# Level products of a chunked gated scan: 64 moving columns in place of 128

## What is computed

```python
def _hgrn2_chunk_scan(q, k, v, log_f):
    """S_t = diag(f_t) S_{t-1} + k_t v_t^T ; o_t = S_t^T q_t."""
    ...
        cum = jnp.cumsum(gi, axis=2)
        o_inter = jnp.einsum('bhtk,bhkv->bhtv', qi * jnp.exp(cum), state)
        diff = cum[:, :, :, None, :] - cum[:, :, None, :, :]
        decay = jnp.exp(jnp.where(causal[:, :, None], diff, -jnp.inf))
        scores = jnp.einsum('bhtk,bhtsk,bhsk->bhts', qi, decay, ki)
        o_intra = jnp.einsum('bhts,bhsv->bhtv', scores, vi)
```

## Time and profile before

| | |
|---|---|
| median of three executions | 3034.97 us |
| the profiled execution, its own time | 3036.25 us |
| its span | 3034.3 us |
| TensorE: matmul records (PE), weight-load records (PEld) | 2937.1 us (97%), 2478.7 us (82%) |
| DVE, ACT, POOL busy | 1331.6, 869.1, 221.3 us |
| mean granted TensorE clock | 0.986 of full speed |

### The profile page before, as it was taken

How to read it: one execution, slowest core, us unless ns; L and a number is a source line. 1 busy time by engine, 2 the same in 40 slices (tenths; PEclk the granted TensorE clock), 3 DMA queues, 4 the chain that set the end, 5 groups by cost and what they waited for, 6 DMA issues and landing times.

```text
span 3034.3 us, 36527 instructions
## 1 busy us (share of the span) xinstructions
PE 2937.1 (97%) x15532; PEld 2478.7 (82%) x15532; DVE 1331.6 (44%) x1674; ACT 869.1 (29%) x1275; POOL 221.3 (7%) x168
## 2 busy tenths in 40 slices
PE   7999999989999999997999999999998999999999
PEld 5888989768888888876988978888876888888887
DVE  6343343555445554336421575674245333333332
ACT  4333343432221111235221243343123222211111
POOL 2121111210000000014100000000011000000000
PEclk8999999999999999998999999999999999999999
DMA  3101101213334432121322301002131111111111
GB/s 121 34 29 36 36 29 36 84 35 118 118 118 125 127 124 69 48 64 63 134 63 70 104 21 35 29 21 91 49 97 35 49 49 49 49 49 49 49 49 63
DMA packets 206450, 198.50 MB, mean 65 GB/s; under 512 B 6224, under 2 KB 187856, under 8 KB 206288
## 3 DMA queue, kind: packets, MB, share of 16 engines
q1 hardware_dynamic: 206288, 196.16, 20.7%
HBM read 182.51 MB, written 13.63 MB: 65 GB/s over the span
## 4 chain that ended last, share of the span: by engine, by line
PE 89%; DVE 5%; ACT 3%; issue 1%; POOL 0%; DMA 0%; SPq 0%; ACTq 0%; DVEq 0%; POOLq 0%
PE ps L399 15%; PE ps L402 15%; PE ps L415 14%; PE ps L603 7%; PE ps L594 7%; PE ps L596 7%; PE ps L485 3%; PE ps L440 3%; PE ps L444 3%; PE ps L442 3%; PE ps L762 2%; DVE HT L1392 2%; PE ps L733 1%; PE ps L745 1%; PE ps L765 1%
## 5 line engine op out<-in xcount | busy, mean ns | idle before, releaser
L1374 DVE TENSOR_TENSOR Wlo<-Wraw,Whi 128x1024 fp32r<-128x1024 f32 x220 | 272.3, 1242 | 1083.4 <-ACT Whi L954 1083.4
L954 ACT ACTIVATE Whi<-Wraw 128x1024 fp32r<-128x1024 f32 x232 | 244.1, 1058 | 1451.3 <-PE ps L415 735.4
L399 PE MATMUL ps<-Hh,Whi 128*128 128x512 f32 x1888 | 595.3, 397 | 23.3 <-ACT Hh L983 14.1
L402 PE MATMUL ps<-Hh,Wlo 128*128 128x512 f32 x1888 | 589.6, 394 | 0.0
L415 PE MATMUL ps<-Hl,Whi 128*128 128x512 f32 x1856 | 453.4, 394 | 4.3 <-DVE Hl L1789 4.2
L399 PEld LDWEIGHTS ps<-Hh,Whi 128*128 128x128 f32 x1888 | 354.8, 190 | 107.6 <-ACT Hh L983 15.8
L402 PEld LDWEIGHTS ps<-Hh,Wlo 128*128 128x128 f32 x1888 | 359.7, 191 | 76.1
L415 PEld LDWEIGHTS ps<-Hl,Whi 128*128 128x128 f32 x1856 | 348.9, 189 | 81.3 <-DVE Hl L1789 5.6
L594 PE MATMUL ps<-ah,Whi 128*128 128x512 f32 x1024 | 398.8, 389 | 1.2 <-ACT ah L1124 1.2
L596 PE MATMUL ps<-ah,Wlo 128*128 128x512 f32 x1024 | 398.4, 389 | 0.0
L603 PE MATMUL ps<-al,Whi 128*128 128x512 f32 x1024 | 253.4, 389 | 0.1
(11 more groups left out here) (259 smaller groups left out, 3379.2 us busy)
## 6 DMA issues: line engine op xcount, KB each, us to landing
Wraw<-in_m_w SPq DMA_DIRECT2D x128, 512.0 KB, 3.9
n<-in_w_ada SPq DMA_DIRECT2D x64, 512.0 KB, 3.6
Wraw<-in_w_in SPq DMA_DIRECT2D x56, 512.0 KB, 4.1
R<-in_xT SPq DMA_DIRECT2D x16, 512.0 KB, 5.0
Wraw<-in_w_gate SPq DMA_DIRECT2D x16, 512.0 KB, 4.5
Wraw<-in_w_out SPq DMA_DIRECT2D x8, 512.0 KB, 4.2
xs_scratch<-R SPq DMA_DIRECT2D x8, 512.0 KB, 3.2
Wraw<-in_dft_d SPq DMA_DIRECT2D x8, 512.0 KB, 4.2
```

What stands on the lines that cost most here:

```text
L399: e.matmul(t[:, c], wh[:, k, ms], opd.hi[:, k, c], start=k == 0, stop=False)
L402: e.matmul(t[:, c], wl[:, k, ms], opd.hi[:, k, c], start=False, stop=False)
L954: e.activation(Whi[n % 4][:], Wraw[n % 2][:], ACT.Copy).then_inc(*S("w_hi").tick(n))
L1374: e.tensor_tensor(Wlo[n % 4][:], Wraw[n % 2][:], Whi[n % 4][:].bitcast(F), ALU.subtract).then_inc(*S("w_lo", "v").tick(n))
```

## The change

Levels 1 to 5 and level 6 become one form: for each of the 8 chunks all 128 keys are the stationary operand, and only the 64 queries of the second halves of the blocks, picked by a strided view (`later`), are the moving one. The products fill 512 columns of PSUM in place of 1024. The masked copies of levels 1 to 5 read 256 columns per call in place of 512, with the same columns of the mask, and write to the second halves in `acc`. Level 6 computes 128 keys by 64 queries per chunk in 8 products in place of 16 small ones, and ACT picks its rectangles out of the wider tile. Levels 0 and 7 stay.

```diff
--- before.py
+++ after.py
@@ -199,6 +199,10 @@
         mc = lambda m0, w0=0: (lambda k: mods[:, m0 + k, w0:w0 + 1])
         c3 = lambda t: t[:].rearrange("p (c m) -> p c m", m=128)
 
+        def later(t, m):
+
+            return t.rearrange("p (b two m) -> p b two m", two=2, m=m)[:, :, 1, :]
+
 
         def cols128(w, c0, rows=1024, r0=0):
             return w[r0:r0 + rows, c0:c0 + 128].rearrange("(k p) c -> p k c", p=P)
@@ -480,14 +484,12 @@
                 else:
                     pe.wait_ge(S("q_mul").at((h, lev - 1)), S("q_copy").at((h, lev - 1)))
                     pe.wait_ge(S("k_mul").at((h, lev - 1)), S("k_copy").at((h, lev - 1)))
-                if m < 32:
+                if lev == 0:
                     for c in range(8):
                         i = e.matmul(c3(ps)[:, c, :], K[:, c, :], Q[:, c, :], start=True, stop=True)
-                elif m == 32:
-                    for b0 in (0, 64):
-                        for c in range(8):
-                            i = e.matmul(ps[b0:b0 + 32, 32 * c:32 * c + 32], K[:, c, b0:b0 + 32],
-                                         Q[:, c, b0 + 32:b0 + 64], start=True, stop=True)
+                elif m <= 32:
+                    for c in range(8):
+                        i = e.matmul(ps[:, 64 * c:64 * c + 64], K[:, c, :], later(Q[:, c, :], m), start=True, stop=True)
                 else:
                     for c in range(8):
                         i = e.matmul(ps[0:64, 64 * c:64 * c + 64], K[:, c, 0:64], Q[:, c, 64:128], start=True, stop=True)
@@ -1058,7 +1060,7 @@
                         act.wait_ge(full_at(("level", h, lev)), out_at(("level", h, 5), 1))
                         for p, b0 in enumerate((0, 64)):
                             e.activation(a3_[b0:b0 + 32, :, b0 + 32:b0 + 64],
-                                         ps[b0:b0 + 32, 0:256].rearrange("p (c t) -> p c t", c=8),
+                                         ps[b0:b0 + 32, 0:512].rearrange("p (c t) -> p c t", c=8)[:, :, 32 * p:32 * p + 32],
                                          ACT.Copy).then_inc(*freed(("level", h, lev), p))
                     elif m == 64:
                         act.wait_ge(full_at(("level", h, lev)), out_at(("level", h, 6), 1))
@@ -1487,8 +1489,17 @@
                                 dve.wait_ge(full_at(("tail", h - 1, 2)))
                             else:
                                 dve.wait_ge(S("acc_zero").at(0))
-                            e.copy_predicated(c3(acc)[:, c, :], masks[:, lev, :][:, None, :].broadcast_to([P, 4, P]),
-                                              c3(ps)[:, c, :]).then_inc(*freed(("level", h, lev), p))
+                            if lev:
+                                nb = T // (2 * m)
+                                to = acc[:].rearrange("p (b two m) -> p b two m", two=2, m=m)
+                                to = to[:, nb // 2 * p:nb // 2 * (p + 1), 1, :]
+                                which = later(masks[:, lev, :], m)[:, None, :, :].broadcast_to([P, 4, nb // 8, m])
+                                to = to.rearrange("p (c b) m -> p c b m", c=4)
+                                of = ps[:, 256 * p:256 * p + 256].rearrange("p (c b m) -> p c b m", c=4, m=m)
+                            else:
+                                to, of = c3(acc)[:, c, :], c3(ps)[:, c, :]
+                                which = masks[:, lev, :][:, None, :].broadcast_to([P, 4, P])
+                            e.copy_predicated(to, which, of).then_inc(*freed(("level", h, lev), p))
                 elif kind == "tail" and i == 1:
                     s3, ps = c3(St), c3(tile(("tail", h, 1)))
                     dve.wait_ge(full_at(("tail", h, 1)))
```

## The result

| | before | with the change |
|---|---|---|
| median | 3036.93 us (11 executions, 3034.79 to 3039.63) | 3043.69 us (11 executions, 3041.46 to 3045.78) |
| ratio, with its 95% interval | | 1.0023 (1.0013 to 1.0032) |
| profiled execution, span | 3034.3 us | 3042.8 us |

The change makes the kernel slower, by 6.8 us between the medians, 4 to 10 us by the interval. Against the three executions known ahead of the prediction, the forecast of 3040.2 us stood for +5.2 us. The measured 3043.7 us lies in the stated range of 3027.5 to 3046.7 us, and in the part of it that belongs to the load as the bound (3036.8 to 3046.7).

A forecast was written before the change was run, and what follows sets the result against it. TensorE was taken to bound the kernel, with pairs bound by the 128-column load. Terms 0 + 5.2 + 0 + 0 = +5.2 us on the three executions' median of 3034.97 gave 3040.2 us, range 3027.5 to 3046.7.

The forecast's parts named there:

- What bounds a pair: TensorE's load and matmul pairs: cost is the longer stream, not the sum; a 128-column load takes about 107 ns.
- The slope of the load records: Load records on TensorE grow 113, 138, 192 ns with width, 0.78 to 0.84 ns a column.
- The pairs with 64 stationary columns: Four pairs with 128 moving columns take 0.44 us, 110 ns each, the price of 128 and 128.
- The third row: Behind level 6, the first full-width pair's matmul of 0.39 us ends 0.11 us later, taken as standing for its load.
- Levels 1 to 5 at 0 us: 40 blocks of 16 pairs stay at 111.5 ns a pair with 64 moving columns: 0 us.
- One of the signs: In blocks of levels 1 to 5 after the change, matmul records near 222 ns would show the prediction right.
- Level 6 at +5.2 us: Level 6's wider products add 0.56 us in four heads, 0.75 in heads 1, 3, 5, 0.7 in head 7.
- The estimate of 473 ns: Each of 80 masked copies in levels 1 to 5 falls from 744 ns to this; 22 us less DVE time, hidden.
- The bound of 744 ns: Upper bound for a halved masked copy, if a stepped view costs double per column; the lower was 372.
- The moving columns as the price: Rival: pairs in levels 1 to 5 cost 67 ns, as at level 7; -28.9 us, 3006.1 us; chance 0.11.
- the mixture: Rival: a pair costs something in between, say 95 ns; -7.5 us, 3027.5 us; chance 0.05.
- The clock: Rival: half-streamed blocks lower the granted clock in head 7; +16.5 us on +5.2, 3056.7 us; chance 0.06.

The follow-up runs named there:

- the second execution of the change: Profiled execution from measuring the unaltered changed kernel again beside the kernel before; that run took 3043.62 us beside 3035.88, ratio 1.0026.
- the kernel with one load for two levels: Kernel before, with odd raw queries and level 2's queries moving over one load, level 1 without own products; 3024.50 us beside 3035.11, ratio 0.9962.

## Why the prediction was right

**What bounds a pair.** The step on which all hung, that the load of 128 columns is the longer stream at 107 ns and the moving side is hidden behind it, held. It rested on three rows, and two of them bore it. The slope of the load records held: inside a block a pair takes 112 ns at 64 and at 32 moving columns, and 58 when the load is halved too, which is 0.84 ns for each stationary column, the slope of the records, and 5 ns on top of the 107 and 53 that the slope alone gives. (The prediction's own 67 ns for level 7 is 1.07 us divided by 16, with the ends of the block in it, and would not have lain on its line.) The pairs with 64 stationary columns held too: 109 ns in the scan. The third row, the matmul behind level 6, was misread. Its record of 0.39 us isn't that of a matmul that stands for its load because little streamed ahead of it: behind 128 stationary and 32 moving columns the record is 0.36 us (at 74.01), the same as behind 128 and 128 (at 75.77), and behind 64 stationary and 128 moving ones it is 0.39. It goes with the narrower stationary operand.

The Trainium skill gives, in TensorE: Matmul & The Clock Gate, section LDWEIGHTS (loading the stationary operand), the columns divided by 1.2 ns, 107 for 128 and 53 for 64 columns; the measured pairs take 5 ns more than that at both widths. The formula in its section Back-to-back issue gap counts the moving columns alone, but the section calls it the gap of isolated matmuls and says that in a stream of load and matmul pairs both set the spacing, which the prediction left out. The runs agree with that: with 128 stationary columns the moving ones, from 128 down to 32, don't change the 112 ns.

**Levels 1 to 5 at 0 us.** Right, and as put: a pair stays at 112 ns, and from projection to projection an even head's block takes 2.02 us for 2.03. In an odd head the projections behind a block give back 0.06 for its 0.05. One of the signs was wrong: I looked for matmul records near 222 ns and they are 275, as long as if 128 columns streamed.

**Level 6 at +5.2 us.** Right: 0.55 us in an even head (0.56), 0.70 in an odd one (0.75), and alone it takes as long as the whole change. The scan holds 5.3 us of the median's 6.8, and the interval takes both in. That three runs gave 6.8, 7.7 and 7.0 us and none less than 5.2 has no account in the prediction; it is no part of what was right.

**The sign.** The chances put 0.62 on a change within 0.2% and 0.23 on slower. The measured ratio is just outside 0.2%. The mechanism that I called the likeliest was there, and in the scan nothing beside it; what set slower against the same was 1 us of the sum at a line of 6.1, with a scatter of the clock between executions that is larger. On which side of the line the result fell was luck.

**The masked copies.** The estimate of 473 ns for each was wrong for two levels out of five, and cost nothing, because it is hidden. The timeline of DVE in head 0 (start, us for two copies), levels 0, 1 and 3:

```profile
70.27 1.38 DVE L1502 COPY_PREDICATED acc<-masks,ps 128x512 f32<-128x512 uint8 x2 [7.89 <-PE ps L489]
...
74.88 1.36 DVE L1502 COPY_PREDICATED acc<-masks,ps 128x256 f32<-128x256 uint8 x2 [0.40 <-PE ps L492]
...
84.20 0.77 DVE L1502 COPY_PREDICATED acc<-masks,ps 128x256 f32<-128x256 uint8 x2 [2.79 <-PE ps L492]
```

In levels 3 to 5, which write runs of 4, 8 and 16 elements of `acc`, two copies take 0.77 to 0.79 us, about what was forecast. In levels 1 and 2, with runs of 1 and 2, half the elements take the full time (1.36 and 1.35 us for two). The bound of 744 ns, given for a stepped view at double the price per column, was the value there. The mean record is 577 ns, and 80 x 167 ns are 13 us of records; as busy time the masked copies go from 66.3 us to 51.3, 15 us less and not 22.

DVE as a whole is only 5.5 us less busy (1326.1 for 1331.6), which the prediction didn't see coming. The gate products of q became longer, before (first line) and after:

```profile
L1477 DVE TENSOR_TENSOR q<-q,Tb 128x512 f32<-128x512 f32 x48 | 34.8, 725 | 8.0 <-PE ps L489 8.0
```

```profile
L1479 DVE TENSOR_TENSOR q<-q,Tb 128x512 f32<-128x512 f32 x48 | 45.4, 945 | 11.8 <-PE ps L492 11.8
```

With the shorter masked copies of levels 3 to 5 they start 0.6 us earlier and then run beside POOL's product of k (in head 0, level 3: DVE from 84.87 for 1.13 us, POOL from 84.34 for 1.12 us; before, DVE from 86.65 for 0.76 us, when POOL's, from 85.50 for 1.11 us, was done). Where level 6 alone is changed the mean stays at 726 ns. That the two engines slow one another is the likeliest reading, but no run tested it. Here it is hidden as well.

**The rivals.** The moving columns as the price and the mixture are ruled out by the two runs with 32 moving and with 64 stationary columns. The clock stayed at 1.00 over the half-streamed blocks and over the quarter-streamed ones, and in the second execution of the change through head 7 as well. Where it was lower, in head 7, a wait of PE stood in front. The prediction's argument that the clock stays at 1.00 behind the wait of 3.2 us rested on one execution and was luck: in the first execution of the change level 0 had 0.53 there.

## What to carry to other kernels

In this kernel, a float32 matmul that brings its own weights costs the longer of two streams, stationary columns and moving columns, so narrowing the side that is not longer gives nothing, and a small product that is widened to share a form pays for the wider load. What a pair costs is read from pairs inside a block; the block's time divided by their number has the ends in it. Before cutting columns, compare the slopes of load and matmul records by width, and look for a row in which the two widths differ. Where the load is the bound, gain lies in loads left out: put everything that the same stationary operand serves behind one load, even if the operands must be prepared for it.

## What was not expected of the hardware

- A masked copy out of PSUM that writes runs of 1 or 2 float32 elements takes as long for 256 columns as one for 512 that writes whole rows (1.36 and 1.38 us for two); with runs of 4 to 16 it takes 0.77 to 0.79 us. In the kernel with one load for two levels, 512 columns in runs of 1 and 2 take 2.72 us for two calls.
- Entering and leaving a block whose stationary operands have 64 columns costs some 0.34 us more than with 128, with 64 moving columns (1.51 us less 16 x 58 ns) as with 128 (2.32 us less 16 x 109 ns). With 128 stationary columns, 128, 64 and 32 moving ones all take 2.02 to 2.03 us from projection to projection.
- Behind the same wait of 3.2 us, the granted clock over the same 16 pairs was 1.00 in two executions and 0.53 to 0.77 in six others, and they took from 2.02 to 3.65 us. A difference of 1 to 2 us between two traces of this program may be no more than that.
- Gate products on DVE took 1.07 to 1.13 us (head 0, behind levels 3 to 5) where POOL's product of k ran beside them, and 0.67 to 0.76 in the kernel before, where it was done.
